# An encoder block with routed experts on one Trainium2 core: expert 0's rows chosen by rank, the merged list turned inside its first products, the last tile worked by column halves

## The reference, cut to what matters

```python
h2 = rms_norm(x, p['norm_ffn'])
logits = jnp.einsum('nd,de->ne', xf, w_router); aff = jax.nn.softmax(logits, axis=-1)
cap = CAPACITY_FACTOR * n // N_EXPERTS                 # 64 tokens for each of 16 experts, per set
gates, idx = lax.top_k(aff.T, cap)                     # each expert picks its 64 best tokens
xe = xf[idx]
hid = jax.nn.silu(einsum(xe, w_gate)) * einsum(xe, w_up)
ye = einsum(hid, w_down) * gates[..., None]
y = zeros_like(xf).at[idx.reshape(-1)].add(ye)         # scattered back, added to x
```

## Time and profile before

| | us |
|---|---|
| median of 3 runs | 1097.08 (1096.93 to 1097.77) |
| the profiled execution's own time | 1097.4 |
| its span in the profile | 1095.6 |
| granted TensorE clock, mean | 0.989 |
| PE busy | 1061.3 (97% of the span) |
| DVE busy | 872.6 (80%) |
| ACT busy | 774.5 (71%) |
| POOL busy | 315.9 (29%) |

### The profile page before, as it was taken

The page is one execution under the profiler, slowest core; times in us unless marked ns, Lnnn a source line. Parts: engine busy times, 40 slices in busy tenths (PEclk is TensorE's granted clock), DMA queues, the critical chain, the costliest instruction groups (busy, mean ns, idle before and its releaser), DMA issues.

```text
span 1095.6 us, 17090 instructions
## 1 busy us (share of the span) xinstructions
PE 1061.3 (97%) x5803; PEld 911.4 (83%) x5803; DVE 872.6 (80%) x1127; ACT 774.5 (71%) x1094; POOL 315.9 (29%) x341
## 2 busy tenths in 40 slices
PE   8999999999999999997799999999999999999996
PEld 7999978999889988886688888888888888888885
DVE  6787769988998843338998898989889898888982
ACT  7655568878888744344677777877777777777772
POOL 2566576111348513334211101111011110111001
PEclk9999999999999999999799999999999999999998
DMA  8232050010211336641799999999999999999982
GB/s 302 83 119 92 1 195 1 1 40 20 97 40 39 97 109 260 231 154 78 278 418 373 407 392 391 389 405 403 392 391 390 408 398 390 394 388 410 398 301 38
DMA packets 72816, 266.04 MB, mean 243 GB/s; under 512 B 6001, under 2 KB 8268, under 8 KB 72508
## 3 DMA queue, kind: packets, MB, share of 16 engines
q1 hardware_dynamic: 65376, 239.68, 56.1%
q0 software_dynamic: 7328, 25.68, 8.2%
q10 hardware_dynamic: 60, 0.01, 0.0%
HBM read 239.07 MB, written 26.28 MB: 242 GB/s over the span
## 4 chain that ended last, share of the span: by engine, by line
PE 49%; DVE 1%; DMA 1%; issue 1%; ACT 0%; POOLq 0%; POOL 0%; DVEq 0%; ACTq 0%
PE ps L1908 10%; PE ps L1910 10%; PE ps L1909 10%; PE ps L1924 5%; PE ps L1922 5%; PE ps L1923 5%; PE ps L1889 3%; DMA out<-y,give 1%; DMA xe<-h,idxT 0%; DVE idx L1710 0%; DVE affT L1713 0%; DVE gates L1708 0%; ACT hi L1995 0%; DVE lo L2065 0%; POOLq L2145 0%
## 5 line engine op out<-in xcount | busy, mean ns | idle before, releaser
L2065 DVE TENSOR_TENSOR lo<-raw,hi 128x2048 fp32r<-128x2048 f32 x191 | 431.8, 2289 | 56.4 <-ACT hi L1995 56.0
L1995 ACT ACTIVATE hi<-raw 128x2048 fp32r<-128x2048 f32 x192 | 364.6, 1918 | 64.9 <-PE ps L1910 58.9
L1908 PE MATMUL ps<-hi,xehi 128*128 128x512 f32 x480 | 188.2, 392 | 0.2 <-DVE h L2077 0.2
L1910 PE MATMUL ps<-hi,xelo 128*128 128x512 f32 x480 | 187.0, 390 | 0.0
L1909 PE MATMUL ps<-lo,xehi 128*128 128x512 f32 x480 | 186.9, 389 | 0.0
L1844 POOL COPY take<-idxT 128x1 uint32 (+1 forms) x15 | 12.7, 848 | 356.6 <-PE ps L1889 356.6
L1908 PEld LDWEIGHTS ps<-hi,xehi 128*128 128x128 f32 x480 | 90.2, 188 | 18.8 <-issue 0.7
L1910 PEld LDWEIGHTS ps<-hi,xelo 128*128 128x128 f32 x480 | 90.1, 188 | 18.7
L1909 PEld LDWEIGHTS ps<-lo,xehi 128*128 128x128 f32 x480 | 90.2, 188 | 18.2
L1345 DVE TENSOR_TENSOR probTlo<-ps,probThi 128x512 fp32r<-128x512 f32 x128 | 87.7, 686 | 16.0 <-ACT probThi L1302 14.1
L1302 ACT ACTIVATE probThi<-ps 128x512 fp32r<-128x512 f32 x128 | 76.7, 599 | 29.4 <-PE ps L1183 29.4
(11 more groups left out here) (277 smaller groups left out, 2134.6 us busy)
## 6 DMA issues: line engine op xcount, KB each, us to landing
raw<-in_w_gate SPq DMA_DIRECT2D x64, 1024.0 KB, 8.2
raw<-in_w_up SPq DMA_DIRECT2D x64, 1024.0 KB, 7.8
raw<-in_w_down SPq DMA_DIRECT2D x64, 1024.0 KB, 8.4
w_raw<-in_w_in SPq DMA_DIRECT2D x8, 592.0 KB, 8.9
x<-in_x SPq DMA_DIRECT2D x8, 512.0 KB, 3.6
woraw<-in_w_o SPq DMA_DIRECT2D x4, 1024.0 KB, 4.8
o<-attention_out SPq DMA_DIRECT2D x8, 512.0 KB, 4.3
xr<-in_x SPq DMA_DIRECT2D x8, 512.0 KB, 6.5
```

The source lines that it names most:

```text
L1908: pe.matmul(ps[:, dst[n], :], rowhi[:, c, :], hi[w][:, cols], start=c == 0, stop=False)
L1910: last = pe.matmul(ps[:, dst[n], :], rowlo[:, c, :], hi[w][:, cols], start=False, stop=c == KD - 1)
L1995: act.activation(hi[s][:], raw[s][:], ACT.Copy).then_inc(hi_done, 1)
L2065: dve.tensor_tensor(lo[s][:], raw[s][:], hi[s][:].bitcast(F32), ALU.subtract).then_inc(lo_done, 1)
```

## The change

Four parts, as the diff has them.

**The last tile by column halves.** Tile 7's second group of products is done for columns 0 to 511 and then 512 to 1023 (`last_product`), each half is added by itself (`add_last`), its transposes, squares and copies follow by halves. The early rounds of the top 64 and the other work of tiles 5 to 7 on DVE and ACT are put in another order; the logits of tile 5 and 6 come one chunk sooner.

**Expert 0's rows by rank.** The rows of tiles before j = 6 are also stored to a second DRAM tensor, `early_h2`. Once the early list stands, PE turns it, DVE makes expert 0's indices from it (`first_index`) and POOL gathers those rows (`fetch_first`). For the two last tiles, DVE compares every token's affinity for expert 0 with every other's (`compare`), PE sums the comparison into a rank (`rank`), DVE makes from rank and bound a 0/1 matrix `late` that says which slot a token takes (`choose`), PE counts the slots taken, and DVE keeps the identity's other columns (`keep`). `first_rows` then forms the transposed rows of expert 0 with three f32 matmuls for each of 8 chunks: the gathered rows times `kept`, and the two tiles' rows, still in SBUF, times `late`. Chunks 0 to 3 are formed ahead of `gate_up(0, 0)`, chunks 4 to 7 behind it.

**Merged list turned later, other rows sooner.** The first late round stands ahead of expert 0's first product, the other seven, `merge` and `indices` run beside it on DVE; PE turns the merged list after `first_rows(4, 8)`. The gather for expert 1 starts as soon as the indices stand, its transposes stand ahead of chunk 6 as before, its split two chunks sooner on ACT and DVE.

**Weights.** The slots are taken in the order `SLOTS = (3, 1, 2, 4, 5, 0)`. Chunks 0 to 2 are split during `route`, `hi` on ACT and `lo` on POOL, the `lo` in place over `raw`, so that their slots come free when PE has used them; POOL also makes the `lo` of chunks 3 and 4. **Identity turned in the ranking:** the 26 turns are gone; 5, 4, 11, 7 and 6 turns stand between the steps of the ranking.

```diff
+SLOTS = (3, 1, 2, 4, 5, 0)
+READY = 3
+        moe["first_lo"] = [Map(arena + s * CHUNK * 4)(f"first_lo{s}", [P, CHUNK], F32R) for s in SLOTS[0:READY]]
 # POOL, route
+            if j == LAST:
+                low(2)
...
+            if u == LAST:
+                fetch_first()
             pool.dma_start(out_rows[ORDER[u]], x1[u % 2][:]).then_inc(x1_stored[u % 2], 16)
+            if u == TS:
+                low(0)
...
+            if u < LAST - 1:
+                pool.dma_start(early_rows(ORDER[u]), rows[:]).then_inc(h2_stored[u % 2], 16)
+            if u == LAST - 2:
+                low(1)
 # PE, route
+            last_product(0, range(GROUP_CHUNKS, KD))
+            last_product(1, range(GROUP_CHUNKS, KD - 1))
+            x_transposes(LAST, 0)
+            last_product(1, range(KD - 1, KD))
+            spread_affinities(0)
+            turn_identity(5)
+            x_transposes(LAST, 1)
+            logits(LAST, range(4))
+            turn_lists()
+            logits(LAST, range(4, KD))
+            turn_identity(4)
+            spread_bounds()
+            rank(0)
+            spread_affinities(1)
             pair_transposes(LAST)
+            turn_identity(11)
+            rank(1)
+            turn_identity(7)
+            count()
+            turn_identity(6)
 # ACT, route: high(0) at j == TS, then
+            scale_rows(LAST - 2)
+            high(1)
+            o_high(LAST, 1)
+            o_squares(LAST)
+            high(2)
+            x_square(LAST - 1)
...
 # DVE, route
+            top_eight(0, EARLY, 0)
+            add_first(LAST - 1)
+            top_eight(0, EARLY, 1)
+            o_low(LAST, 1)
+            top_eight(0, EARLY, 2)
+            add_second(LAST - 1)
+            for r in range(3, 6):
+                top_eight(0, EARLY, r)
+            add_first(LAST)
+            logit_bias(LAST - 1)
+            add_last(0)
+            affinities(LAST - 1)
             top_eight(0, EARLY, 6)
+            largest(0, EARLY, 7)
+            add_last(1)
+            find(0, EARLY, 7)
...
+            first_index()
             logit_bias(LAST)
+            compare(0)
             affinities(LAST)
+            choose(0)
+            compare(1)
+            choose(1)
+            largest(1, LATE, 0, AT)
+            keep()
+            find(1, LATE, 0, AT)
 # SP, experts
         for j in range(RING, GU_CHUNKS):
-            load(0, j, GATE_UP[j % 2], 0, j // 2)
+            sp.wait_ge(chunk_used, j - RING + 1)
+            load_chunk(sp, a, moe, raw_loaded, slot_of(0, j), GATE_UP[j % 2], 0, j // 2)
+        sp.wait_ge(chunk_used, READY)
 # PE, experts
+            for c in range(c0, c1):                    # first_rows
+                pe.matmul(ps[:, bank, at:at + P], pick["rows"][:, cols], pick["kept"][:], start=True, stop=False)
+                for n in range(SETS):
+                    last = pe.matmul(ps[:, bank, at + n * CAP:at + (n + 1) * CAP], wo["late"][n][:, cols],
+                                     pick["late"][:, n * CAP:(n + 1) * CAP], start=False, stop=n == SETS - 1)
-        for _ in range(26):
-            pe.transpose(ps[:, G[0], 0:P], k["ident"][:], k["ident"][:])
+        first_rows(0, 2, pick_turned)
+        first_rows(2, 4, xt_ready)
+        pe.wait_ge(pick_done, DONE["late read"])
+        gate_up(0, 0)
+        first_rows(4, KD, xt_ready)
+        turn_merged()
+        for i in range(1, 4):
+            gate_up(0, i)
 # DVE, experts
+        for r in range(1, 4):
+            late_round(r)
+        low_pair(0, pick_copied, COPIED["rows ahead"], pick_done)
+        late_round(4)
+        low_pair(2, xehi_done, 1, xelo_done)
+        for r in range(5, CAP // 8):
+            late_round(r)
+        merge()
+        indices()
+        low(htlo, hthi, 1, xehi_done, 2, xelo_done)
+        dve.wait_ge(lo_done, RING - 1)
+        split(0, RING - 1)
```

More of the change, by code:

```diff
@@ L1428, in route @@
     lmax_done, nbias_done, lexp_done, lrec_done, aff_done = sem("lmax_done"), sem("nbias_done"), sem("lexp_done"), sem("lrec_done"), sem("aff_done")
+    hi_done, lo_done, xe_loaded = sem("hi_done"), sem("lo_done"), sem("xe_loaded")
+    rules_ready, pick_turned, pick_copied, pick_done = (sem(n) for n in ("rules_ready", "pick_turned", "pick_copied", "pick_done"))
+    RULES_READY = 5
+    value = lambda *names: {n: i + 1 for i, n in enumerate(names)}
+    TURNED = value("spread 0", "lists", "bounds", "rank 0", "spread 1", "rank 1", "count", "rows ahead")
+    COPIED = value("bounds", "rows ahead")
+    DONE = value("early list", "index 0", "index 1", "before 0", "late 0", "before 1", "late 1", "kept", "late read", "rows ahead")
     at_ready, at_done, merged, psteps, vsteps = sem("at_ready"), sem("at_done"), sem("merged"), sem("pool_steps_r"), sem("vector_steps_r")
@@ L1535, in x_transposes, with logits @@
             last.then_inc(x1t_ready, 1)
-        def logits(j):
-            if j:
+        def logits(j, chunks=range(KD)):
+            if j and chunks[0] == 0:
                 pe.wait_ge(lexp_done, j)
@@ L1557, in rest, with rank, count @@
+        def rank(n):
+            pe.wait_ge(pick_done, DONE[f"before {n}"])
+            pe.matmul(rank_ps(n), pick["before"][n][:], pick["ones"][:], start=True, stop=True).then_inc(pick_turned, 1)
+        def count():
+            pe.wait_ge(pick_done, DONE["late 1"])
+            pe.matmul(count_ps, pick["late"][:], pick["ones"][:], start=True, stop=True).then_inc(pick_turned, 1)
         def rest():
             for j in range(T):
-                for c in range(KD):
+                for c in range(KD if j < LAST else GROUP_CHUNKS):
@@ new lines, in choose, with keep @@
+        def choose(n):
+            dve.wait_ge(pick_turned, TURNED[f"rank {n}"])
+            if n == 0:
+                dve.wait_ge(pick_turned, TURNED["bounds"])
+            steps.did(dve.tensor_scalar(pick["place"][:], place_ps, rank_ps(n), None, ALU.is_equal))
+            steps.wait()
+            dve.scalar_tensor_tensor(out=late_of(n), in0=bound_ps(n), scalar=affinity(n), in1=pick["place"][:],
+                                     op0=ALU.is_lt, op1=ALU.mult).then_inc(pick_done, 1)
+        def keep():
+            dve.wait_ge(pick_turned, TURNED["count"])
+            dve.tensor_scalar(pick["kept"][:], ident_ps, count_ps, None, ALU.is_gt).then_inc(pick_done, 1)
@@ L1903, in gate_up @@
                 pe.wait_ge(lo_done, at(e, j) + 1)
+                low = low_of(e, j)
+                if first and j == GU_CHUNKS - 2:
+                    second_rows()
                 for kk in range(2):
```

412 lines of the change are left out of this document (278 added, 134 removed).

## The result

| | before | after |
|---|---|---|
| median, us (16 runs each) | 1097.37 (1096.86 to 1097.9) | 1100.7 (1098.94 to 1104.36) |
| ratio to before | | 1.0034, 95% interval 1.0028 to 1.004 |
| span of the profiled execution | 1095.6 | 1100.2 |

The change made the kernel 0.34% slower, with an interval that leaves out 1, and its runs lie 5.4 us apart instead of 1.0. The forecast was 1093.9, its range 1090.2 to 1098.2.

What follows compares the result with a forecast made beforehand. PE was taken to bound the experts' stage, with a nearly idle hole ahead of it. PE going on 3.2 us sooner behind expert 0, other terms 0, gave 1094.2, median 1093.9; range 1090.2 to 1098.2.

Steps and rivals of the forecast that it cites:

- Up to the last affinities: Work before the last tile's affinities: priced at 0, bounds 0.3 us gained and 1.5 us lost.
- Affinities to product: From the last affinities to expert 0's first product: 18.4 us become 8.0, start at 524.75.
- the clock falls in the ranking and is back for the products: Rival, chance 0.28: slower turns in the ranking, start 526.75, gain 1.2 us, time 1095.9.
- The records of `first_rows`: PE's f32 matmuls forming expert 0's rows: 24 ahead of the first product, taken at 0.108 us each.
- Expert 0: PE's stretch on expert 0: 22.5 us become 25.4, with 2.6 for `first_rows(4, 8)` and 0.15 for the merged list's transposes.
- The product behind it: PE's wait in expert 1 for `product(0)`: stands still 4.9 us, goes on at 557.8 against 560.99, gaining 3.2 us.
- DVE's sum: DVE's own work up to the product behind expert 0: done at 555.5; alone it would give 5.4 us gained.
- The clock's rivals: Two rivals: clock low in the ranking only (0.28, 1095.9), or still low at expert 0's products (0.12, 1099.1).
- No stall: Rival, chance 0.12: behind expert 0, DVE and loads are there in time, gain 6.8 us, time 1090.3.
- Slower with the clock still low at expert 0's products: Rival, chance 0.12: start at 528.5, first 3 us of products at half speed, 5.2 us added, time 1099.1.
- The transfer alone: Rival, chance 0.03: weight chunk 12 lands as late as before, near 555; no change, 1097.

Runs made afterwards that it cites:

- the turn ahead of the rows: Changed kernel with the merged list turned right behind expert 0's first products, rows of chunks 4 to 7 later, chunk 5's split sooner; 1098.32 us, ratio 1.0005.
- both orders mended: Changed kernel with expert 0's product ahead of the last two splits and the merged list turned right behind the first products; 1091.52 us, ratio 0.9941.

## Why the prediction was wrong, point by point

**Up to the last affinities: 0.** Gained were 1.2 us, outside the bound of 0.3: the last residual ended at 511.4 (its second half 510.69 to 511.41) where it had ended at 512.57, but not by the halves: 0.85 of it was there already at tile 6's residual, which ended at 499.55 where the forecast had 500.4, so the new order of DVE's work cost less than was placed for it. `high(2)` did wait for the stores (2.36 us) and held nothing up: it ended at 499.58, and `x_square(6)` began at 499.65.

**Affinities to product: 8.0 us.** Measured: 10.5 us (515.52 to 526.06), which takes the 1.2 us back and 1.3 more. It is the clock: in the one profile of this order in which the clock did not fall in the ranking, that of the turn ahead of the rows, the same way took 7.9 us (515.81 to 523.67). The rival "the clock falls in the ranking and is back for the products" came true at this point: 526.75 was its start, 526.06 was measured. Its time, 1095.9, was not met. The records of `first_rows`, 0.112 us each (24 in 2.6 to 2.7 us), were sized right.

**Expert 0: 25.4 us.** Measured: 25.9 (526.06 to 551.94, one record of 0.227 behind 551.71). 0.2 of the 0.5 us is the mark: 557.64 in the earlier trace rows is a weight load, and by the mark used here PE left expert 0 at 557.86. Of the rest, `first_rows(4, 8)` took 2.7 us and the merged list's transposes 0.2.

**The product behind it: the step that failed.** The forecast named the place, the wait and the chain, and had the load of chunk 12 decide, not DVE's sum. That was right. What failed is the size of one term, chunk 8's landing at 541, on which chunk 12's hangs; it came at 545.67:

| | forecast | measured | off by |
|---|---|---|---|
| first product | 524.75 | 526.06 | 1.3 |
| chunk 8 asked for | 535.7 | 538.08 | 2.4 |
| chunk 8 there (its split starts) | 541 | 545.67 | 4.7 |
| chunk 12 there | 552.2 | 556.94 | 4.7 |
| PE goes on | 557.8 | 562.52 | 4.7 |

Of the 4.7 us, 1.3 are the later start (the ranking's clock, less the 1.2 us gained ahead of it), 1.1 lie between the first product and the issue (0.4 in PE's products and rows, 0.65 from the end of chunk 2's products at 537.44 to SP's issue), and 2.3 the transfer: 7.6 us from issue to split instead of 5.3. The transfer's part is shown by holding the loads back (5.3 us). The issue's is read from the trace alone, since the run with the turn ahead of the rows moves other work too. Behind chunk 8 the forecast's pace held: 11.27 us for four chunks against 11.2.

**The clock behind the stand: the second step that failed, a term put at nothing without a reason.** The forecast had PE standing still for 4.9 us and priced the stand alone. Nothing in it asked what clock PE would find afterwards. Measured, it cost 2.4 us on 12 matmuls and 0.4 on the transposes, and in the runs above it fell behind stands of 3.58 and 3.33 us as well. The clock's rivals were both put at expert 0's start. So the sum, 3.2 us gained, lost 4.7 and 2.8 more, which leaves 4.3 us of loss where the spans show 4.6. Turns of the identity in the stand took the second part away, and the product ahead of the last splits took both.

**The rivals.** No stall: came true only with both orders mended, at 1091.5 where 1090.3 was worked out. Slower with the clock still low at expert 0's products: right sign, wrong place; when that clock was in fact low there, in the three kernels without the turns, the median moved by -0.9, +0.8 and +1.6 us and not by 5.2. The transfer alone, 1097: the load of chunk 12 did decide, as in the forecast too, and the price stopped too early: PE went on 1.5 us later than before instead of at the same time, and the clock behind the stand came on top. Against a case without a stall the forecast had DVE's own sum 1.7 us too late; its own bounds, 5.4 and 6.8 us, give 1.4.

**The turns.** Here 45 turns held the clock at 2.4 GHz over 5.08 us where PE standing still lost it. Against that, it fell between 514 and 516 in five of the seven profiles that have the turns among PE's work in the ranking. The Trainium skill (TensorE: Matmul & The Clock Gate, Part 4, PE-mode transpose) says that transposes don't count as PE busy for the clock the same way as other work, and that the full clock does not engage for them. The rule as it stands is not borne out by the first, and the second does not settle it.

**Open.** What makes the changed kernel scatter over 5.4 us is not shown. It does not go with the stand. The five kernels that have the turn of the merged list ahead of the rows lie within 1.2 to 2.1 us (4 to 10 runs each), the one with the stand of 3.58 us among them; the kernels of the change without that order spread over 2.8 to 8.9 us (4 to 16 runs), the one with the product first and no such stand too (3.8). Which part of that order does it was not run. The clock is one part of the scatter: in the changed kernel the five runs with a mean granted clock of 0.992 took 1098.9 to 1100.7 us, the three with 0.989 took 1102.1 to 1103.8, but the slowest, 1104.4, had 0.990.

## What to carry to other kernels

When a stage is made to start sooner, follow what its loads and its successors' loads wait for: here the later gates of the loads and one order of splits turned a start 9 us sooner into an end of the stretch 1.5 us later, and the clock added 2.8. Look then at what stands behind a late load in an engine's own order without needing it; a product that PE waits for belongs ahead of splits that PE doesn't need yet. And price a new stand of TensorE twice, once for itself and once for the clock behind it.

## What the runs showed of the hardware that was not expected

- A stand of TensorE of 3.3 to 6.3 us between full products brought the clock to 1.2 GHz in four kernels, and 5.6 to 6.0 us of work passed at that clock before it was back (562.52 to about 568.5 in the changed kernel, 561.24 to 567 in the one with the later loads). Behind stands of 1.1 us ahead of expert 1 it did not fall.
- The same instructions in the ranking got a different clock from one profile to the next: low from 514 to about 521 (first product at 526.06, 526.08, 526.09), low from 515 to about 518.5 (524.74, 525.14), or not low at all (523.67). Where it did not fall in the ranking or came back soon, it fell in the first products instead in three profiles, and in one (first product at 522.21, with the first low part sooner) not at all. Ahead of the first product PE had stood 1.5 us in those three and 0.42 us in that one; but it had stood 1.5 us, without a fall, in the three in which the clock had been low until 521.
- With six loads of 1 MB asked for within 5.3 us, the first needed 7.6 us and the fifth 15.7; with at most two under way the first needed 5.3. For the loads asked for from 525 to 560, issue to landing went from 4.8/8.4/10.7 us (least, median, most) to 5.4/11.1/16.0; over the whole kernel the median did not rise (8.1, 7.8 after).
